# Moving both adaLN products of the first layer's opening onto TensorE in column form

## The chip, the cores and the metric

The kernel runs on one core of a Trainium2 chip. The metric is device microseconds (us) of one launch; lower is better. The engines are TensorE (PE, with its weight loads as PEld), VectorE (DVE), ScalarE (ACT), GpSimd (POOL) and SyncE (SP), which here only issues transfers.

## The reference

A trunk of two transformer layers over 256 tokens of width 2048, batch 1, in float32. Each layer has a mixer (layer 0: sparse attention and latent attention side by side; layer 1: forgetting attention) and a SwiGLU network; in front of each stands an RMS norm that the condition `c` modulates. What the change touches is the first of these norms:

```python
cond = silu(c)                                   # (1, 2048)
mod = (cond @ ada_w[i] + ada_b[i])[:, None, :]   # ada_w[i]: (2048, 6*2048)
sh1, sc1, g1, sh2, sc2, g2 = jnp.split(mod, 6, axis=-1)
h = rmsnorm(x, norm_mix[i]) * (1.0 + sc1) + sh1
...                                              # layer 0: y = nsa_mla_mixer(h, ...), first h @ w_in
x = x + g1 * y
h = rmsnorm(x, norm_ffn[i]) * (1.0 + sc2) + sh2
x = x + g2 * swiglu(h, ffn_w1[i], ffn_w3[i], ffn_w2[i])
```

So before the first projection can begin, two products of `cond` with a 2048 x 2048 slice of `ada_w[0]` are needed: the scale `sc1` and the shift `sh1`, 16 MB each.

## The kernel before

All weights stream once from HBM, in units of 1 MB (128 partitions x 2048 floats), through a ring `RAW` of four slots. `Plan` in `make_plan` numbers the units in the order in which SP loads them: kind "w" is a weight unit, "a" a k-tile of `ada_w` that DVE multiplies and adds, "r" one that PE reads raw. `load` waits, before it fills a slot again, until the unit that was in it four units ago has been used (`lo_ready` for w, `ada_used` for a, `row_used` for r).

A weight unit is split in two for float32 precision: ACT writes the rounded part `WHI` (L554), DVE the rest `WLO` (L1427). The activations are split in the same way into `AHI` and `ALO`. A product is then three matmuls of 128x128 by 128x512 (L909, L910, L911) per k-tile and block of 128 tokens. A chunk is 512 output columns, so four weight units.

An "a" unit costs DVE one instruction of 128x2048: `ACC += RAW * COND[kt]` (L1437 for the first k-tile, L1440 for the others). The 16 k-tiles leave 128 partial sums per column, and PE adds them over the partitions: in `finish` for a shift or scale with 16 matmuls of 128x128 by 128x1 (L958, the accumulator as stationary operand, a column of ones as the moving one), for a gate with four matmuls of 128x128 by 128x512 (L954).

The prologue is 32 units, "a" and "r" in turn. The "a" units make the shift (0, SH1) on DVE. The "r" units make the scale (0, SC1) on PE as a row: `COND[:, k]` (128x1) is stationary and four pieces of 128x512 of the unit move (L1100). Between them stand the six pieces of the position bias: DVE compares (`steps`, L1584, 16 small instructions), PE looks up (`bias_piece`, L1091), DVE keeps (L1592). After the last unit DVE copies the row out of PSUM (L1609), PE turns it into a column with 16 matmuls of one partition (L1106), PE sums the shift (L958), DVE makes `SHM` and `GS` (L1460 to L1468), then the inverse root of the mean square of x (L1511 to L1529). Then `norm(0)` works in four groups of 512 columns: ACT scales x (L669), PE transposes it (L973), DVE modulates (L1536), ACT and DVE split it (L565, L1525). Only after the fourth group does ACT begin on the first two weight units.

The first projection `even_in` has seven chunks of four weight units and an eighth (`even_in`, 7) of 88 columns in one unit. Each chunk carries two "a" units of the gate (0, G1), 16 in all; the last two lie in chunk 7. Then `finish((0, G1))` on PE waits for all 16, and DVE adds the sums to `GROW` (L1451). After it come the turned gates (L1122, L1650), the compression's input (L1660) and its products (L1130).

Every trace record counts a float32 matmul with N=512 or N=1 of plain (unsplit) type as two passes; the order of instructions lists it once. So L958's 16 matmuls are x32 in the trace.

Of the kernel before, what the change touches and what calls it, by code (L numbers as in the profile page):

```python
# [25 lines left out]
RING = 4  # L26
# [40 lines left out]
class Unit:  # L67

    def __init__(self, kind, s, n, w_before, a_before, r_before, src=None, nk=0, cols=0, kt0=0):
        self.kind, self.s, self.n, self.w_before, self.a_before, self.r_before = kind, s, n, w_before, a_before, r_before  # L70
        self.src, self.nk, self.cols, self.kt0 = src, nk, cols, kt0
        if kind == "a":
            self.vec, self.kt = ADA_ORDER[n]
# [31 lines left out]
class Plan:  # L105
# [15 lines left out]
    def chunk(self, name, i, weights, ada=0, buf=None):  # L121

        units, done = [], 0
        for j, (src, nk, cols, kt0) in enumerate(weights):
            units.append(self.unit("w", src=src, nk=nk, cols=cols, kt0=kt0))
# [39 lines left out]
class Machine:  # L165

    def __init__(self, nc, t, ctx, known):
# [74 lines left out]
        self.DG = self.L[:, 0, 0, 0:256].rearrange("p (b t) -> p b t", b=2)  # L242
        self.PART = self.RS[:, 2, 4:6]
# [27 lines left out]

    def scaled_rows(self, g):
# [11 lines left out]
    def make_plan(self, t):  # L284
        plan = self.plan = Plan()

        def rows(w, cols, n, per=4, tiles=KT):
# [9 lines left out]
        self.even_in.append(plan.chunk("even_in", 7, [  # L297
            (tuple(win[:, a:b].rearrange("(k p) n -> p k n", p=P) for a, b in ((2560, 2584), (3608, 3672))), KT, 88, 0)], 2))
# [37 lines left out]
        assert plan.a == len(ADA_ORDER) and plan.r == KT + 8  # L336
# [8 lines left out]
        order = [("norm", 0, g) for g in range(4)] + [("even_in", i) for i in range(7)] + [("cmp", 0), ("cmp", 1)]  # L345
# [27 lines left out]
    def sum_bank(self, v):  # L373

        return {(0, SH1): 5, (0, SC2): 7}.get(v, 6)

    def staged_by(self, key):

        return "st_copied" if key[0] in ("norm", "cmp", "mla") or key in [("even_in", i) for i in range(5)] else "st_ready"

    def t_freed_by(self, key):

        if key[0] == "norm" and key[1]:
            return ("tf_ready", key + (None,))
        if key[0] in ("norm",) or key in (("even_in", 5), ("even_in", 6)):
# [13 lines left out]
def sync_program(block, nc, t, out, m):  # L399

    @block.sync
    def _(sp):
        kinds = m.plan.kinds

        def load(u):
# [9 lines left out]
            if u.src is None:  # L415
                (layer, seg), kt = (u.vec, u.kt) if u.kind == "a" else (ADA_ROW, u.n)
# [42 lines left out]
        for at, src in ((V_C, t["c"].rearrange("a (k p) -> (a k) p", p=P)),  # L459
                        (V_MIX, t["norm_mix"].rearrange("a (k p) -> (a k) p", p=P)),  # L460
                        (V_FFN, t["norm_ffn"].rearrange("a (k p) -> (a k) p", p=P)),
                        (V_QN, t["mla_q_norm"].rearrange("a (k p) -> (a k) p", p=P)),
                        (V_KVN, t["mla_kv_norm"].rearrange("a (k p) -> (a k) p", p=P)),
                        (V_FQ, t["fox_q_norm"]), (V_FK, t["fox_k_norm"]), (V_PK, t["nsa_cmp_pos_k"][0])):
            m["vec_full"].tick(sp.dma_start(m.VROWS[0][at:at + src.shape[0], :], src), "all", 16)
        m["vec_full"].tick(sp.dma_start(m.VROWS[1][0:32, :], t["nsa_cmp_pos_v"][0]), "all", 16)
        for i in range(2):
            m["vec_full"].tick(sp.dma_start(m.VROWS[2 + i][0:96, :], t["ada_b"][i].rearrange("(k p) -> k p", p=P)), "all", 16)
        for u in m.prologue[:RING]:
            load(u)  # L470
        pos = t["positions"]
        m["pos_full"].tick(sp.dma_start(m.POST_I, pos[0:1, :].to_broadcast([P, T])), "all", 16)
        m["pos_full"].tick(sp.dma_start(m.PI[:], pos[0].rearrange("(b p) -> p b", p=P), allow_slow_non_contiguous=True), "all", 16)
        for g in range(4):
            m["pos_full"].tick(sp.dma_start(m.RB[32 * g:32 * g + 32, :], t["rel_bias"][:, :]), "all", 16)
        sp.wait_ge(m["zeroed"].sem, m["zeroed"].at("shifted"))
        for g in range(4):
            m["pos_full"].tick(sp.dma_start(m.RBS[32 * g + 1:32 * g + 32, :], t["rel_bias"][0:31, :]), "all", 16)
        for tb in range(2):
            m["x_full"].tick(sp.dma_start(m.X[:, tb, :], t["x"][0, P * tb:P * tb + P, :]), "all", 16)  # L480
        m["x_full"].tick(sp.dma_start(m.GB[:], t["nsa_gate_b"][0:1, :].to_broadcast([P, 24])), "all", 16)
        m["x_full"].tick(sp.dma_start(m.FB[0:16, 0:1], t["fox_f_b"].rearrange("a h -> h a"), allow_slow_non_contiguous=True), "all", 16)
        for u in m.prologue[RING:]:
            load(u)
        load_chunks(m.even_in)
# [47 lines left out]
def scalar_program(block, nc, t, out, m):  # L533

    @block.scalar
    def _(act):
# [122 lines left out]
        def norm(n):  # L659
            root(("norm", n), 2)  # L660
            wait("rs_ready", n)

            def scaled(g):
                if g >= 2:
                    wait("t_done", ("norm", n, g - 2))
                elif ("norm", n, 0) in m.before_batch:
                    wait("t_done", m.before_batch[("norm", n, 0)])
                for tb in range(2):
                    m["st_copied"].tick(A((m.ST, m.S2)[g % 2][:, tb, :], m.X[:, tb, 512 * g:512 * g + 512], ACT.Copy,  # L669
                                          scale=m.RS[:, 3, tb:tb + 1]), ("norm", n, g))  # L670
            scaled(0)
            scaled(1)
            for g in range(4):
                wait("tf_ready", ("norm", n, g))
                split_hi(("norm", n, g), m.AHI[:, 4 * g:4 * g + 4, :], m.TF[:])
                if g < 2:
                    scaled(g + 2)

        wait("vc_ready", 0)
        m["silu_done"].tick(A(m.COND[:], m.VC[:, V_C:V_C + KT], ACT.Silu), "cond")  # L680
        wait("ang_ready", 0)
        m["trig_ready"].tick(A(m.SIN[:], m.ANG[:, 0:2, :], ACT.Sin), 0)
        m["trig_ready"].tick(A(m.COS[:], m.ANG[:, 2:4, :], ACT.Sin), 0)
        wait("x_full", "all")
        for i in range(4):
            x_squares(("norm", 0), i)
        norm(0)

        def even_first(c):  # L690
# [5 lines left out]
            if c.i < 5:  # L696
                wait("t_done", m.before_batch[c.key])
# [196 lines left out]
def tensor_program(block, nc, t, out, m):  # L894

    @block.tensor
    def _(pe):
# [148 lines left out]

        def run(chunks, stat, ready, after=lambda c: None, rows=(0, 1), between=lambda c, j: None):

            for i, c in enumerate(chunks):
# [5 lines left out]
                for j, u in enumerate(c.w):  # L1055
                    if out and c.i == 3 and j >= len(c.w) - 2:
                        if j == len(c.w) - 2:
                            last_two(c, lambda u: stat(c, u), lambda j: [ready(c, j)])
                        continue
# [13 lines left out]
        def norm(n):  # L1073
            for g in range(4):
                staged(("norm", n, g), range(0, 512, P), g % 2, (m.ST, m.S2)[g % 2])

# [7 lines left out]
        def bias_piece(q):  # L1085
            wait("oh_ready", q)
            if q >= 2:
                wait("bias_kept", q - 2)
            for i in range(16):
                for a in range(3):  # L1090
                    ins = mm(m.PS[:, 6 + q % 2, 32 * i:32 * i + 32], m.OH[q % 2][:, i, :], m.TBL[:, a].rearrange("p g h -> p (g h)"),  # L1091
# [3 lines left out]

        wait("silu_done", "cond")
        for k, u in enumerate(m.prologue[1::2]):
            pe.wait_ge(m.raw_full[u.s % RING], 16 * (u.s // RING + 1))
            for q in range(4):
# [1017 lines left out]
```

## Time and profile before

| | us |
|---|---|
| median of 3 runs | 2775.75 (2767.36 to 2777.0) |
| the profiled execution, own time | 2772.71 |
| its span | 2770.8 |
| first product of `even_in` starts | 154.96 |
| PE busy | 2581.2 (93%) |
| DVE busy | 1720.6 (62%) |
| ACT busy | 1020.1 (37%) |

The profiled execution is one run; its own time is 1.9 us above its span and 3.0 us below the median. Busy shares are of the whole span; the prologue is the first 155 us, and the groups of rows below are taken from it and from a few later places where the same instructions stand. The granted TensorE clock is given as a share of full speed: 1.00 is 2.4 GHz, 0.50 is 1.2 GHz.

### The profile page before, as it was taken

The numbers are of one execution on the slowest core, as the hardware profiler recorded it, in microseconds if no ns is written. First come the engines' busy times: TensorE is split into PE (matmuls) and PEld (weight loads), VectorE is DVE, ScalarE is ACT, GpSimd is POOL, SyncE is SP. The second block draws the span as 40 slices with busy tenths as digits, with TensorE's granted clock in tenths as the row PEclk, the third lists the DMA queues.
The fourth block names the chain that finished last, engine by engine and source line by source line (L and its number), as shares of the span: only waits on it lengthen the run. The fifth ranks groups of instructions, "written<-read, shape, count | busy, mean of one in ns | idle before, by whom it ended". The sixth has DMA issues, their size and how long they took to land.

```text
span 2770.8 us, 29298 instructions
## 1 busy us (share of the span) xinstructions
PE 2581.2 (93%) x11766; PEld 2066.2 (75%) x11766; DVE 1720.6 (62%) x1398; ACT 1020.1 (37%) x947; POOL 3.2 (0%) x11
## 2 busy tenths in 40 slices
PE   5789877889999999999997999999999999999998
PEld 1368656567787788878876888878778788888886
DVE  6566637485766766676656666677677654445445
ACT  1033213244433333333344444444443333333333
POOL 0000000000000000000000000000000000000000
PEclk8789978699999999999998999999999999999999
DMA  8758645476687778777876888789678755655553
GB/s 316 284 203 283 199 151 211 152 257 214 234 312 281 265 251 304 268 268 250 296 215 142 230 183 214 188 237 316 225 252 297 262 187 182 196 182 196 183 185 118
DMA packets 255001, 636.54 MB, mean 230 GB/s; under 512 B 16858, under 2 KB 28084, under 8 KB 229428
## 3 DMA queue, kind: packets, MB, share of 16 engines
q1 hardware_dynamic: 254180, 629.89, 69.2%
q0 software_dynamic: 720, 5.24, 0.5%
q8 instruction: 71, 1.16, 0.2%
q14 instruction: 30, 0.25, 0.0%
HBM read 633.00 MB, written 2.10 MB: 229 GB/s over the span
## 4 chain that ended last, share of the span: by engine, by line
PE 83%; DVE 9%; DMA 3%; ACT 2%; issue 2%; SPq 1%; DVEq 0%; ACTq 0%
PE PS L909 24%; PE PS L911 24%; PE PS L910 24%; DVE WLO L1427 3%; DMA RAW<-in_ada_w 2%; DVE ACC L1440 1%; ACT WHI L554 1%; PE PS L1100 1%; PE PS L958 1%; PE PS L973 1%; PE PS L1130 1%; PE PS L954 1%; PE PS L1287 1%; PE PS L1331 1%; DMA RAW<-in_mla_w_ukv 1%
## 5 line engine op out<-in xcount | busy, mean ns | idle before, releaser
L909 PE MATMUL PS<-WHI,AHI 128*128 128x512 f32 x2120 | 835.2, 394 | 27.6 <-DVE WLO L1427 11.3
L911 PE MATMUL PS<-WHI,ALO 128*128 128x512 f32 x2120 | 828.2, 391 | 0.0
L910 PE MATMUL PS<-WLO,AHI 128*128 128x512 f32 x2120 | 827.7, 390 | 0.0
L1427 DVE TENSOR_TENSOR WLO<-RAW,WHI 128x2048 fp32r<-128x2048 f32 (+2 forms) x222 | 503.6, 2270 | 392.7 <-ACT WHI L554 392.3
L554 ACT ACTIVATE WHI<-RAW 128x2048 fp32r<-128x2048 f32 (+2 forms) x222 | 421.2, 1898 | 709.4 <-PE PS L911 650.2
L1921 DVE TENSOR_TENSOR WLO<-RAW,WHI 128x2048 fp32r<-128x2048 f32 x176 | 403.4, 2292 | 361.7 <-ACT WHI L788 361.1
L788 ACT ACTIVATE WHI<-RAW 128x2048 fp32r<-128x2048 f32 x176 | 337.4, 1917 | 590.9 <-PE PS L911 571.0
L909 PEld LDWEIGHTS PS<-WHI,AHI 128*128 128x128 f32 x2120 | 400.0, 189 | 114.4 <-issue 26.7
L911 PEld LDWEIGHTS PS<-WHI,ALO 128*128 128x128 f32 x2120 | 399.5, 188 | 84.2
L910 PEld LDWEIGHTS PS<-WLO,AHI 128*128 128x128 f32 x2120 | 399.6, 188 | 81.0 <-issue 0.2
L909 PE MATMUL PS<-WHI,GHI 128*128 128x512 f32 x960 | 382.1, 398 | 16.2 <-DVE GLO L1525 8.4
L911 PE MATMUL PS<-WHI,GLO 128*128 128x512 f32 x960 | 377.9, 394 | 0.0
L910 PE MATMUL PS<-WLO,GHI 128*128 128x512 f32 x960 | 377.6, 393 | 0.0
L1440 DVE SCALAR_TENSOR_TENSOR ACC<-RAW,COND,ACC 128x2048 f32<-128x2048 f32 x109 | 255.6, 2345 | 9.5 <-DMA RAW<-in_ada_w 8.3
L909 PEld LDWEIGHTS PS<-WHI,GHI 128*128 128x128 f32 x960 | 183.1, 191 | 59.1 <-DVE GLO L1525 10.5
L911 PEld LDWEIGHTS PS<-WHI,GLO 128*128 128x128 f32 x960 | 182.5, 190 | 38.7
L910 PEld LDWEIGHTS PS<-WLO,GHI 128*128 128x128 f32 x960 | 182.7, 190 | 37.8 <-issue 0.5
L1932 DVE SCALAR_TENSOR_TENSOR ACC<-RAW,COND,ACC 128x2048 f32<-128x2048 f32 x60 | 140.7, 2346 | 0.1
L1100 PE MATMUL PS<-RAW,COND 128*1 128x512 f32 x128 | 65.1, 662 | 31.7 <-DMA RAW<-in_ada_w 31.6
L1100 PEld LDWEIGHTS PS<-RAW,COND 128*1 128x1 f32 x128 | 10.5, 89 | 80.6 <-issue 46.9
L725 ACT ACTIVATE L<-L,NM 128x128 f32<-128x128 f32 x80 | 35.4, 444 | 89.3 <-DVE NM L1729 89.2
L973 PE MATMUL PS<-CON,ST 128*128 128x128 f32 (+1 forms) x244 | 35.9, 290 | 17.9 <-ACT ST L669 6.8
(289 smaller groups left out, 1519.3 us busy)
## 6 DMA issues: line engine op xcount, KB each, us to landing
RAW<-in_ffn_w SPq DMA_DIRECT2D x264, 1024.0 KB, 5.2
RAW<-in_ada_w SPq DMA_DIRECT2D x192, 1024.0 KB, 5.6
RAW<-in_fox_w_in SPq DMA_DIRECT2D x64, 1024.0 KB, 8.6
RAW<-in_even_w_in SPq DMA_DIRECT2D x28, 1024.0 KB, 5.3
RAW<-in_even_w_out SPq DMA_DIRECT2D x16, 1024.0 KB, 6.0
RAW<-in_fox_w_out SPq DMA_DIRECT2D x16, 1024.0 KB, 6.3
GROW<-in_ada_b POOLq DMA_DIRECT2D x4, 1024.0 KB, 5.5
RAW<-in_nsa_cmp_w_k SPq DMA_DIRECT2D x4, 1024.0 KB, 6.3
```

The lines of the kernel that those rows point to most:

```text
L554: A(m.w_view(m.WHI, u), m.w_view(m.RAW, u), ACT.Copy).then_inc(m["hi_ready"].sem, 1)
L725: m["exp_done"].tick(A(m.L[:, b, h, cols], m.L[:, b, h, cols], ACT.Exp, bias=m.NM[:, b, j:j + 1], accum_out=m.SM[:, b, j:j + 1]), p)
L788: A(m.WHI[:, (up.w0 + j) % 2, :], m.RAW[:, (up.s0 + s) % RING, :], ACT.Copy).then_inc(m["hi_ready"].sem, 1)
L909: mm(dst(tb), xh, whi[:, k, :], start=first and k == 0, stop=False)
L910: mm(dst(tb), xh, wlo[:, k, :], start=False, stop=False)
L911: ins = mm(dst(tb), xl, whi[:, k, :], start=False, stop=last and k == nk - 1)
L973: ins = turn(dst, src, m.CON[0:n, C_ID:C_ID + n])
L1100: ins = mm(m.PS[0:1, q, :], m.COND[:, k:k + 1], m.RAW[:, u.s % RING, 512 * q:512 * q + 512], start=k == 0, stop=k == KT - 1)
L1427: TT(m.w_view(m.WLO, u), m.w_view(m.RAW, u), m.w_view(m.WHI, u).bitcast(F32), ALU.subtract).then_inc(m["lo_ready"].sem, 1)
L1440: STT(out=acc[:], in0=raw, scalar=m.COND[:, kt:kt + 1], in1=acc[:], op0=ALU.mult, op1=ALU.add).then_inc(m["ada_used"].sem, 1)
L1921: TT(m.WLO[:, (up.w0 + j) % 2, :], m.RAW[:, (up.s0 + s) % RING, :], m.WHI[:, (up.w0 + j) % 2, :].bitcast(F32), ALU.subtract).then_inc(m["l ...
L1932: STT(out=m.ACC[:], in0=m.RAW[:, slot, :], scalar=m.COND[:, col], in1=m.ACC[:], op0=ALU.mult, op1=ALU.add).then_inc(m["ada_used"].sem, 1)
```

## The change

Nothing but the first norm and the places of a few units is changed.

* All 32 units of the prologue are "r": for each k-tile the scale's, then the shift's. PE takes each in column form: 16 blocks of 128x128 of the unit are stationary, `COND[:, kt]` (128x1) moves, and the sums of all 32 units gather in 32 columns of one PSUM bank. DVE's 16 multiply-adds, the copy of the row, its turning (L1106) and the summing of the shift (L958) are gone.
* x is transposed raw, after units 8 and 14 (`x_raw`), and multiplied by its inverse root on DVE into `XG`, beneath the loads; `spread_both` brings the root into rows of 128 partitions with one matmul.
* The bias pieces stand after units 16, 18, ... 26 and use one PSUM bank instead of two.
* The first two weight units are loaded ahead of the last four "r" units, and split before the modulation.
* After the last unit DVE makes `SHM` and `GS`, and modulation and split go k-tile by k-tile; `opening_unit` on PE waits for one k-tile at a time.
* The small inputs are loaded from ACT's queue, not from SP's; x follows the first four units.
* The 16 "a" units of (0, G1) stand in chunks 0 to 6 as 2, 2, 2, 3, 3, 2, 2, and chunk 7 has none.

```diff
-        self.prologue = [plan.unit("ar"[k % 2]) for k in range(2 * KT)]
-        self.even_in = [plan.chunk("even_in", i, rows(win, 512 * i + (24 if i > 4 else 0), 512), 2) for i in range(7)]
+        self.prologue, self.opening = [], []
+        for kt in range(KT):
+            if kt >= KT - 2:
+                src, nk, cols, kt0 = rows(win, 0, 512)[kt - (KT - 2)]
+                self.opening.append(plan.unit("w", src=src, nk=nk, cols=cols, kt0=kt0))
+                self.prologue.append(self.opening[-1])
+            self.prologue += [plan.unit("r", vec=(0, seg), kt=kt) for seg in (SC1, SH1)]
+        self.even_in = [plan.chunk("even_in", i, rows(win, 512 * i + (24 if i > 4 else 0), 512), (2, 2, 2, 3, 3, 2, 2)[i],
+                                   early=self.opening if i == 0 else ()) for i in range(7)]
...
 # PE
+        side = {8: lambda: (x_raw(0), x_raw(1)), 10: spread_both, 14: lambda: (x_raw(2), x_raw(3))}
+        side.update({16 + 2 * q: lambda q=q: bias_piece(q) for q in range(6)})
+        for k, u in enumerate([u for u in m.prologue if u.kind == "r"]):
             pe.wait_ge(m.raw_full[u.s % RING], 16 * (u.s // RING + 1))
-            for q in range(4):
-                ins = mm(m.PS[0:1, q, :], m.COND[:, k:k + 1], m.RAW[:, u.s % RING, 512 * q:512 * q + 512], start=k == 0, stop=k == KT - 1)
-            m["row_used"].tick(ins, k)
-            if k % 2 and 3 <= k <= 13:
-                bias_piece((k - 3) // 2)
-        wait("row_kept", 0)
-        for j in range(KT):
-            ins = mm(m.PS[:, 4, j:j + 1], m.XT[0:1, j // 2, P * (j % 2):P * (j % 2) + P], m.ONE[0:1, 0:1], start=True, stop=True)
-        m["row_turned"].tick(ins, 0)
-        finish((0, SH1))
-        wait("modulated", 0)
-        norm(0)
+            for j in range(KT):
+                at = KT * (u.vec[1] == SH1) + j
+                ins = mm(m.PS[:, 6, at:at + 1], m.RAW[:, u.s % RING, P * j:P * j + P], m.COND[:, u.kt:u.kt + 1],
+                         start=k == j == 0, stop=k == 2 * KT - 1 and j == KT - 1)
+            m["row_used"].tick(ins, ("ada", k))
+            if k in side:
+                side[k]()
...
+        def opening_unit(c, j):
+            u = c.w[j]
...
+            pe.wait_ge(m["lo_ready"].sem, u.n + 1)
+            for k in range(4):
+                kt = u.kt0 + k
+                wait("lo_split", ("norm", 0, kt))
...
 # ACT
+        for u in m.opening:
+            hi(u)
+        wait("gs_ready", 0)
+        for kt in range(KT):
+            m["hi_split"].tick(A(m.AHI[:, kt, :], m.XG[:, kt, :], ACT.Identity, scale=m.GS[:, 0, kt:kt + 1], bias=m.SHM[:, 0, kt:kt + 1]), ("norm", 0, kt))
...
 # DVE
+        for u in m.opening:
+            lo(u)
+        wait("row_used", ("ada", 2 * KT - 1))
+        modulate(0, SH1, 0, m.PS[:, 6, KT:2 * KT])
+        modulate(0, SC1, 0, m.PS[:, 6, 0:KT])
+
+        def modulated(kt):
+            if kt >= 4:
+                wait("lo_split", ("norm", 0, kt - 4))
+            m["tf_ready"].tick(TS(m.TF[:, kt % 4, :], m.XG[:, kt, :], m.GS[:, 0, kt:kt + 1], m.SHM[:, 0, kt:kt + 1], ALU.mult, ALU.add), ("norm", 0, kt))
+        modulated(0)
+        for kt in range(KT):
+            if kt + 1 < KT:
+                modulated(kt + 1)
+            wait("tf_ready", ("norm", 0, kt))
+            split_lo(("norm", 0, kt), m.ALO[:, kt, :], m.TF[:, kt % 4, :], m.AHI[:, kt, :])
```

How PE's instructions stand in a row from its first transposes to the first product. The kernel before; L1100 is the scale's row, L1091 the bias, L1106 the row's turning, L958 the shift's sums:

```order
L1081 MATMUL PS<-CON,TF 128x96 x2
L1100 MATMUL PS<-RAW,COND 1x512 x16
L1091 MATMUL PS<-GROW,ST 128x32 x48
L1100 MATMUL PS<-RAW,COND 1x512 x8
...
L1100 MATMUL PS<-RAW,COND 1x512 x16
L1106 MATMUL PS<-CON,XT 128x1 x16
L958 MATMUL PS<-CON,ACC 128x1 x16
L973 MATMUL PS<-CON,ST 128x128 x8
L973 MATMUL PS<-CON,S 128x128 x8
...
L909 MATMUL PS<-WHI,AHI 128x512
```

PE at the same place after the change; L1133 is the column form of scale and shift, L1119 the transposes of x, L1124 the spreading of the root, L1105 the bias:

```order
L1095 MATMUL PS<-CON,TF 128x96 x2
L1133 MATMUL PS<-COND,RAW 128x1 x144
L1119 MATMUL PS<-CON,X 128x128 x16
L1133 MATMUL PS<-COND,RAW 128x1 x32
L1124 MATMUL PS<-L,CON 128x256
L1133 MATMUL PS<-COND,RAW 128x1 x64
L1119 MATMUL PS<-CON,X 128x128 x16
L1133 MATMUL PS<-COND,RAW 128x1 x32
L1105 MATMUL PS<-GROW,ST 128x32 x48
...
L1133 MATMUL PS<-COND,RAW 128x1 x80
L1058 MATMUL PS<-WHI,AHI 128x512
```

Sixteen units of four wide matmuls have become 32 units of 16 matmuls of one column; the row's turning and the transposes of the scaled x no longer stand between the last unit and the first product.

On DVE, after the change, from the last kept bias piece to the first units of the projection (L1605 and L1625 bias, L1454 `WLO`, L1637 modulation, L1552 `ALO`, L1464 and L1467 the gate's "a" units):

```order
L1605 COPY BIAS<-PS 128x64x8 x2
L1625 TENSOR_TENSOR BIAS<-BIAS,CON 128x8x128 x2
L1454 TENSOR_TENSOR WLO<-RAW,WHI 128x2048 x2
L1487 TENSOR_TENSOR SHM<-PS,VC 128x16
L1489 COPY IDLE<-SHM 128x1
L1493 TENSOR_TENSOR MD<-PS,VC 128x16
L1495 SCALAR_TENSOR_TENSOR GS<-MD,VC 128x16
L1637 TENSOR_SCALAR TF<-XG,GS,SHM 128x256 x2
L1552 TENSOR_TENSOR ALO<-TF,AHI 128x256
...
L1464 TENSOR_SCALAR ACC<-RAW,COND 128x2048
L1454 TENSOR_TENSOR WLO<-RAW,WHI 128x2048 x2
```

The two weight units are split ahead of the modulation, and the third weight unit waits behind all 16 k-tiles and one "a" unit.

## Rows read from the trace of the kernel before

**Rows 1.** The page: granted TensorE clock in 40 equal slices of the span.
```profile
PEclk8789978699999999999998999999999999999999
```
**Rows 2.** Windows: start:end, length, busy PE, PEld, DVE, ACT, POOL (count), clock, DMA, GB/s.
```profile
40.00:110.00 70.00, 57.14 (x391) 15.65 (x390) 55.02 (x99) 0.00 (x0) 0.00 (x0) 0.94 0.95 373
115.50:121.20 5.70, 5.70 (x32) 5.70 (x32) 0.00 (x0) 0.00 (x0) 0.00 (x0) 0.61 1.00 407
121.20:128.20 7.00, 7.00 (x33) 6.92 (x33) 0.00 (x0) 0.00 (x0) 0.00 (x0) 0.50 0.06 23
128.20:155.00 26.80, 7.65 (x34) 6.49 (x33) 17.03 (x35) 13.04 (x15) 0.00 (x0) 0.50 0.00 0
155.00:157.50 2.50, 2.50 (x6) 2.02 (x7) 2.50 (x2) 0.00 (x0) 0.00 (x0) 0.50 0.62 146
157.60:180.00 22.40, 22.40 (x100) 18.50 (x99) 9.74 (x5) 7.35 (x4) 0.00 (x0) 1.00 0.78 281
```
**Rows 3.** Windows of L958 alone, the column form, at three places.
```profile
121.20:128.20 7.00, 6.97 (x32) 6.90 (x32) 0.50 0.06 23
520.30:527.30 7.00, 6.99 (x32) 6.90 (x32) 0.50 0.44 152
1377.80:1381.50 3.70, 3.63 (x32) 3.54 (x31) 1.00 1.04 385
```
**Rows 4.** Windows of all engines: L958 after dense products, and what follows it.
```profile
1437.40:1441.00 3.60, 3.60 (x34) 3.60 (x33) 2.45 (x2) 2.80 (x4) 0.00 (x0) 1.00 1.03 163
1441.00:1444.00 3.00, 3.00 (x9) 2.39 (x9) 2.64 (x3) 0.44 (x2) 0.00 (x0) 0.53 1.01 149
```
**Rows 5.** Timeline from the last unit to the first product: start, length, engine, line.
```profile
109.46 3.59 PE L1100 MATMUL PS<-RAW,COND 128*1 128x512 f32 x8 [1.43 <-DMA RAW<-in_ada_w]
...
128.26 0.17 DVE L1460 TENSOR_TENSOR SHM<-PS,VC 128x16 f32<-128x16 f32 x1 [12.82 <-PE PS L958]
...
129.07 0.15 DVE L1614 COPY MD<-GS 128x1 f32<-128x1 f32 x1
...
132.44 1.94 PE L973 MATMUL PS<-CON,ST 128*128 128x128 f32 x8 [4.22 <-ACT ST L669]
...
136.35 1.06 ACT L565 ACTIVATE AHI<-TF 128x1024 fp32r<-128x1024 f32 x1 [2.83 <-DVE TF L1536]
137.51 1.23 DVE L1525 TENSOR_TENSOR ALO<-TF,AHI 128x1024 fp32r<-128x1024 f32 x1 [1.19 <-ACT AHI L565]
...
154.96 0.77 PE L909 MATMUL PS<-WHI,AHI 128*128 128x512 f32 x1 [9.87 <-DVE WLO L1427]
```
**Rows 6.** Timeline: the start, a bias piece, and DVE in the first chunk.
```profile
5.63 2.07 SPq L417 DMA_DIRECT2D RAW<-in_ada_w  x4
...
9.19 0.22 ACT L680 ACTIVATE COND<-VC 128x16 f32<-128x16 f32 x1 [7.16 <-DVE VC L1545]
...
13.24 9.28 PE L1100 MATMUL PS<-RAW,COND 128*1 128x512 f32 x16 [4.72 <-DMA RAW<-in_ada_w]
...
46.09 1.36 PE L1091 MATMUL PS<-GROW,ST 128*128 128x32 bf16 x48
...
156.93 1.28 DVE L1437 TENSOR_SCALAR ACC<-RAW,COND 128x2048 f32<-128x2048 f32 x1
164.03 2.29 DVE L1427 TENSOR_TENSOR WLO<-RAW,WHI 128x2048 fp32r<-128x2048 f32 x1 [5.83 <-ACT WHI L554]
```
**Rows 7.** Timeline of DVE at the end of `even_in`.
```profile
324.70 4.80 DVE L1440 SCALAR_TENSOR_TENSOR ACC<-RAW,COND,ACC 128x2048 f32<-128x2048 f32 x2
329.42 0.41 DVE L1622 COPY TF<-PS 88x256 f32<-88x256 f32 x1
...
336.11 0.69 DVE L1451 TENSOR_TENSOR GROW<-PS,GROW 128x512 f32<-128x512 f32 x1 [0.34 <-PE PS L954]
```
**Rows 8.** Timeline of PE at the same place.
```profile
319.64 1.04 PE L973 MATMUL PS<-CON,ST 128*128 128x128 f32 x8
329.56 6.51 PE L954 MATMUL PS<-ACC,CON 128*128 128x512 f32 x8 [8.88 <-DVE ACC L1440]
```

More of the change, by code:

```diff
@@ L458, in _ @@
         m["con_full"].tick(sp.dma_start(m.CON[:], t["const_table"][:, :]), 0, 16)
[L459 to L468, printed above, removed]
         for u in m.prologue[:RING]:
             load(u)
[L471 to L478, printed above, removed]
         for tb in range(2):
             m["x_full"].tick(sp.dma_start(m.X[:, tb, :], t["x"][0, P * tb:P * tb + P, :]), "all", 16)
[L481 to L482 removed]
         for u in m.prologue[RING:]:
             load(u)
[L485 removed]
+        for c in m.even_in:
+            for u in c.units:
+                if u not in m.opening:
+                    load(u)
         for u in m.cmp_in[0]:
@@ L657, in enter @@
             keep_x(n, 3)
[L659 to L677, printed above, removed]
+        for at, src in ((V_C, t["c"].rearrange("a (k p) -> (a k) p", p=P)),
+                        (V_MIX, t["norm_mix"].rearrange("a (k p) -> (a k) p", p=P)),
+                        (V_FFN, t["norm_ffn"].rearrange("a (k p) -> (a k) p", p=P)),
+                        (V_QN, t["mla_q_norm"].rearrange("a (k p) -> (a k) p", p=P)),
+                        (V_KVN, t["mla_kv_norm"].rearrange("a (k p) -> (a k) p", p=P)),
+                        (V_FQ, t["fox_q_norm"]), (V_FK, t["fox_k_norm"]), (V_PK, t["nsa_cmp_pos_k"][0])):
+            m["vec_full"].tick(act.dma_start(m.VROWS[0][at:at + src.shape[0], :], src), "all", 16)
@@ L681, in _ @@
+        wait("x_full", "all")
+        for i in range(4):
+            x_squares(("norm", 0), i)
+        root(("norm", 0), 2)
         wait("ang_ready", 0)
@@ L1093, in bias_piece, with x_raw, spread_both @@
             m["bias_sum"].tick(ins, q)
+        def x_raw(g):
+            if g == 0:
+                wait("x_full", "all")
+            if g >= 2:
+                wait("xg_ready", g - 2)
+            for j in range(4):
+                for tb in range(2):
+                    at = 512 * g + P * j
+                    ins = turn(m.x_turned(g)[:, j, P * tb:P * tb + P], m.X[:, tb, at:at + P], m.ID)
+            m["t_done"].tick(ins, ("norm", 0, g))
+        def spread_both():
+            wait("diag_ready", 0)
+            m["spread_done"].tick(mm(m.PS[:, 5, 0:T], m.ONE, m.DGF, start=True, stop=True), 0)
@@ L1115, in even_after @@
                 staged(c.key, (0, P) if c.i in (3, 4) else range(0, 512, P))
-        run(m.even_in, lambda c, u: halves(m.AHI, m.ALO, u.kt0), lambda c, j: ("lo_split", ("norm", 0, j)), even_after)
+        run(m.even_in, lambda c, u: halves(m.AHI, m.ALO, u.kt0), lambda c, j: None, even_after)
         finish((0, G1))
@@ L1648, in _ @@
         wait("gk_turned", 0)
+        wait("bias_full", "all")
         gk = m.PS[:, 4, 0:T].rearrange("p (b n) -> p b n", b=2)
```

116 lines of the change are left out of this document (61 added, 55 removed).

## The prediction

> **What bounds the kernel now.** I read the page first. The granted clock in 40 slices shows that the kernel is a PE kernel with a weak spot at its beginning: the first three slices and the sixth to eighth are at 8 tenths or below [rows 1]. The prologue is the first 155 us, so it has to be read by itself, in windows. From 40 to 110 us the 16 DMA engines are 95% busy at 373 GB/s, PE is busy for 57 of 70 us and DVE for 55: the loads bound that part [rows 2]. At 373 GB/s a unit of 1.05 MB takes 2.8 us, so the 32 units can't be had in less than 90 us. From 113 us on the transfers no longer matter (23 GB/s, then none), and what runs is a chain: the last row unit ends at 113.05, the first product starts at 154.96, 41.9 us later [rows 2, 5]. In that chain PE stands at half clock from the row's turning to the first product and 2.5 us beyond [rows 2].
>
> The change takes that chain out, and pays for it with work on PE: that is the trade to be costed.
>
> **The column form, the term that decides.** A unit in row form is 8 passes and takes 3.59 us at full clock [rows 5]. The column form of a unit is 16 matmuls of 128x128 by 128x1, in 32 passes. It is not in the prologue before, but the same instruction is: L958 sums an accumulator of 128x2048 with a column of ones, with the same shapes and types. It takes 3.63 us at full clock and 6.97 to 6.99 at half [rows 3]. So at full clock a column unit costs what a row unit costs, and everything hangs on the clock.
>
> What does the clock do under this form? In 115.5 to 121.2 PE is busy all the time with L1106 (one column moving), the window begins partly at full clock (0.61 in the mean), and the clock falls and stays at 0.50 through the 7.0 us of L958 that follow without a gap [rows 2]. That is 12.7 us of an engine that is 100% busy by the record, and the clock is not raised. At 520.3 the same: 7.0 us at 0.50 [rows 3]. Where L958 comes on a fast PE it runs at 3.6 us, and the clock is at 0.53 in the 3 us behind it, though dense products run there [rows 4]. So no row shows this form raise the clock, and two show it lost. Against this the dense products: half clock at 155.0 to 157.5, full from 157.6 [rows 2]. In the changed kernel nothing dense stands before or between the 32 units. I take half clock for all of them: 32 x 6.99 = 223.7 us. The other end is 32 x 3.63 = 116.2 us.
>
> The Trainium skill speaks against this reading: by "TensorE: Matmul & The Clock Gate", Part 1, the engine's own recent busyness releases the throttle, and column units in an unbroken row leave no idle time. By that the term would be the 116 us of the other end. The two windows at 115.5 and 121.2 don't agree with it, busy throughout and at half. It is the first rival below.
>
> **The rest of PE's row.** Four batches of eight transposes: 1.94 us each at half clock [rows 5], 7.8 us. The root's spreading: one matmul of 256 columns, two passes, about half a row-form pass of 0.85 us at half clock each (the first 16 passes took 9.28 us, mostly at half [rows 6]): 0.9 us. Six bias pieces: 1.36 us each at full clock [rows 6]; at half clock the trace has none. They are no cheaper than 1.36 and, since every other PE form doubles, no dearer than 2.7; I take 2.0, between, since 48 matmuls of 32 columns at 28 ns are partly bound by issue: 12.0 us, with ends 8.2 and 16.3. Each piece also waits for DVE, but two column units (14 us) lie between pieces, and DVE's part is one keep of 1.0 and 16 compares of 4.2 us: hidden.
>
> The start: before, `COND` is ready at 9.41 and PE begins on the first row unit at 13.24, when its load has landed [rows 6]. Now the loads are issued some 4 us before their 5.63 [rows 6], since SP issues the constants and then them, and the small inputs compete with them from ACT's queue. Not before 9.4, not after 16; I take 12.0, near the 13.24. The loads themselves are no bound at 6.99 us a unit against 2.8.
>
> Sum: 12.0 + 223.7 + 7.8 + 0.9 + 12.0 = 256.4 us for the end of the last unit, where 113.05 was. This is 143 us later.
>
> **The chain behind it.** `SHM` and `GS` take 0.8 us (128.26 to 129.07) [rows 5]. Then ACT's 128x256 `AHI`: a quarter of the 1.06 us form plus a fixed part, 0.4; DVE's `ALO`, from the 1.23 us form, 0.4 [rows 5]. The weight units are split already. First product at 256.4 + 1.7 = 258.1, where 154.96 was: **+103.1 us**. The 41.9 us of the chain are gained but for 1.7; the 143 us more than eat them.
>
> Behind the first product: DVE now has 16 times a modulation (about 0.3) and a split (0.4), 11 us, before the "a" unit (1.28) and `WLO` of the third weight unit (2.29) [rows 6]: ready 14.4 us after the first product. PE's first two units are 48 products, 2.5 us at half clock and the rest at 0.227, 12.2 us (0.227 from 100 passes in 22.4 us from 157.6 on [rows 2]). PE waits **+2.2 us**; ends 0 and 4. Before, it did not wait there.
>
> At the end of `even_in` PE stands idle for 8.88 us [rows 8] until DVE has done the two last "a" units (4.80 us), which start at 324.70 behind the second split; then PE's sums take 6.51 us [rows 8], and DVE's last addition ends at 336.80 [rows 7]. Those two units are now in chunks 3 and 4, where DVE has room: it is busy 9.7 of 22.4 us in the first chunk [rows 2], and a third "a" adds 2.35. So PE can begin at 320.7, after its transposes [rows 8]; the first two sums wait for nothing, the last two for DVE's additions after 324.7 + 0.4: 325.1 + 4 x 0.7 and two handovers, about 328.5. **-8.3 us**; ends 0 (if the compression's weights or a later DVE step are late next) and -10.
>
> Sum against the span: 103.1 + 2.2 - 8.3 = +97.0; 2770.8 + 97.0 = 2867.8, and with the 1.9 us around the span 2869.7. The median of before is 3.0 above the profiled time, so the forecast of **2870** could be met from 2870 to 2873 by that alone.
>
> **The rivals.** *Full clock throughout.* Continuous column work holds PE at 1.00, as in the 3.6 us of 1437.4 and 1377.8 [rows 3, 4]. Then 12.0 + 116.2 + 4 x 0.9 + 0.4 + 8.2 = 140.4, first product 142.1: -12.9. The opening runs fast from the start, 10.9 us against DVE's 14.4, a wait of 3.5 less 1.3 won: +2.2. With -8.3: -19.0, a time of 2754, faster. It decides from the point where the clock is granted for over about 85% of the units. For it: the full-clock rows of L958. Against it: they begin on a clock that was high already, and one is followed at once by a fall.
>
> *Lifts.* Bias pieces and transposes, dense in columns for a moment, raise the clock for a while. If each of the eight side batches gives one column unit at 3.63 instead of 6.99, 27 us are won: 2843; with two each, 54: 2816. Against it: eight transposes twice (132.4 to 136.1) and all of `norm(0)` lie in 128.2 to 155.0 at 0.50 [rows 2, 5].
>
> *DMA-bound as now.* The units follow the loads at 2.8 us, the sum is 12 + 90, first product near 110. Both prices of the column unit are above 2.8, so I give it nothing.
>
> **How the numbers follow.** Half clock throughout 0.83, lifts 0.08, full clock 0.09. The forecast's own range: start -2.6 to +4, bias -3.8 to +4.3, opening -2.2 to +1.8, end of `even_in` -1.7 to +8.3, so 2859 to 2888, and up to 3 us for the median. Down to 2842 it takes in the mildest lifts; full clock and the strong lifts stay out, some 14 in 100. Range 2842 to 2892. Over 0.5% (14 us), about what a measurement of this kernel can tell from no change: faster 0.09, same 0.01, slower 0.90.
>
> **What would show it.** In the changed profile: the column form x1024 in the first 257 us, about 218 ns a pass, granted clock 0.50 in that window; DMA share near 0.4 there, at 150 GB/s; DVE and ACT mostly idle; the last unit to the first product 1.7 us; the sums of (0, G1) directly behind their transposes. Wrong if the column passes come at 113 ns (the first rival) or if the clock rises after a bias piece (the second); if units take longer than 7 us, then they wait for something that I have not named.

## The result, and the profile after

The changed kernel takes 2857.85 us (median of 4 runs, 2852.24 to 2869.15) against 2776.38 us before (4 runs): a ratio of 1.0305, 95% interval 1.0264 to 1.0346. It is slower by 81 us. The forecast was 2870, with a range of 2842 to 2892. The profiled execution took 2869.15 us with a span of 2867.4, 96.6 us above the span of before.

The prologue in the timeline of the chain that ended last; columns are start, length, engine, line. It answers to [rows 5] and [rows 6]:

```profile
5.10 10.31 DMA TF<-in_ada_b
15.55 1.20 PE PS L1095 x4
16.85 0.53 DVE VC L1558
17.67 61.60 PE PS L1133 x288
79.27 3.52 PE PS L1119 x16
82.78 13.44 PE PS L1133 x64
96.23 1.06 PE PS L1124 x2
97.29 27.10 PE PS L1133 x128
124.39 3.52 PE PS L1119 x16
127.90 13.44 PE PS L1133 x64
141.35 1.30 PE PS L1105 x48
142.65 13.63 PE PS L1133 x64
...
216.01 1.30 PE PS L1105 x48
217.32 34.12 PE PS L1133 x160
252.28 0.66 DVE TF L1637 x2
253.56 0.77 PE PS L1058
```

From 17.67 us on every piece is PE's own, with no wait between: 288 passes in 61.60 us are 213.9 ns a pass, 6.84 us a unit. That is the half-clock price of [rows 3]. All 1024 passes of L1133 take 217.9 us, 6.81 us a unit in the mean. The transfers set the pace before, at 373 GB/s [rows 2]. From 17.7 to 251.4 us they now give 156 GB/s in the mean, at a DMA share of 0.44; at the end, where the first weight units are loaded too, it is 0.68 (windows of all engines; busy us of PE, PEld, DVE, ACT, POOL, then clock, DMA share, GB/s):

```profile
17.70:78.90 61.20, 61.20 (x287) 61.20 (x288) 16.39 (x78) 8.18 (x21) 0.00 (x0) 1.00 0.43 147
217.10:251.40 34.30, 34.30 (x169) 34.24 (x164) 7.97 (x5) 1.91 (x1) 0.66 (x1) 1.00 0.68 244
```

From the last unit to the first product the timeline shows what the change was made of, and it works as written:

```profile
251.46 0.17 DVE L1487 TENSOR_TENSOR SHM<-PS,VC 128x16 f32<-128x16 f32 x1 [18.06 <-PE PS L1133]
...
252.07 0.17 DVE L1495 SCALAR_TENSOR_TENSOR GS<-MD,VC 128x16 f32<-128x16 f32 x1
252.28 7.99 ACT L687 ACTIVATE AHI<-XG,SHM,GS 128x256 fp32r<-128x256 f32 x16 [21.20 <-DVE GS L1495]
252.28 0.73 DVE L1637 TENSOR_SCALAR TF<-XG,GS,SHM 128x256 f32<-128x256 f32 x2
252.98 0.43 DVE L1552 TENSOR_TENSOR ALO<-TF,AHI 128x256 fp32r<-128x256 f32 x1
```

The last unit ends at 251.4 and the first product starts at 253.56: 2.1 us where 41.9 us stood. The chain that the change removes is really gone. It is outweighed by a prologue that ends 138 us later.

At the end of `even_in` the long wait of [rows 8] is cut in two, one short piece of work on each side of a smaller wait (PE; the bracket is idle time before and who ended it):

```profile
420.46 1.88 PE L954 MATMUL PS<-ACC,CON 128*128 128x512 f32 x4
425.92 3.58 PE L954 MATMUL PS<-ACC,CON 128*128 128x512 f32 x4 [3.57 <-DVE GROW L1478]
```

### The profile page after: what moved, and what is told of

It is laid out like the page before. It is cut to its first block, busy times and chain, and to the rows that moved or that the text cites. A ratio compares the mean times of both kernels' runs of the same rounds, so it can differ in the third digit from the quotient of the medians.

```text
span 2867.4 us, 30943 instructions
## 1 busy us (share of the span) xinstructions
PE 2726.7 (95%) x12600; PEld 2267.2 (79%) x12600; DVE 1686.1 (59%) x1398; ACT 1021.8 (36%) x953; POOL 3.2 (0%) x11
## 4 chain that ended last, share of the span: by engine, by line
PE 87%; DVE 8%; ACT 2%; issue 1%; DMA 1%; ACTq 0%; SPq 0%; DVEq 0%
PE PS L909 23%; PE PS L911 23%; PE PS L910 23%; PE PS L1133 8%; DVE WLO L1454 2%; ACT WHI L549 1%; DVE ACC L1467 1%; PE PS L973 1%; PE PS L1157 1%; PE PS L958 1%; PE PS L1314 1%; PE PS L1358 1%; PE PS L1210 1%; PE PS L954 1%; DMA RAW<-in_mla_w_ukv 0%
## 5 line engine op out<-in xcount | busy, mean ns | idle before, releaser
L909 PE MATMUL PS<-WHI,AHI 128*128 128x512 f32 x2088 | 821.7, 394 | 19.8 <-DVE ALO L1908 9.6
L911 PE MATMUL PS<-WHI,ALO 128*128 128x512 f32 x2088 | 814.4, 390 | 0.0
L910 PE MATMUL PS<-WLO,AHI 128*128 128x512 f32 x2088 | 814.3, 390 | 0.0
L1454 DVE TENSOR_TENSOR WLO<-RAW,WHI 128x2048 fp32r<-128x2048 f32 (+2 forms) x222 | 503.7, 2270 | 389.7 <-ACT WHI L549 389.4
L909 PEld LDWEIGHTS PS<-WHI,AHI 128*128 128x128 f32 x2088 | 393.2, 188 | 104.8 <-issue 16.5
L911 PEld LDWEIGHTS PS<-WHI,ALO 128*128 128x128 f32 x2088 | 392.9, 188 | 82.6
L910 PEld LDWEIGHTS PS<-WLO,AHI 128*128 128x128 f32 x2088 | 393.1, 188 | 79.5 <-issue 0.2
L1467 DVE SCALAR_TENSOR_TENSOR ACC<-RAW,COND,ACC 128x2048 f32<-128x2048 f32 x94 | 220.5, 2345 | 0.4 <-issue 0.3
L1133 PEld LDWEIGHTS PS<-COND,RAW 128*128 128x128 f32 x1024 | 219.5, 333 | 1.4 <-ACT COND L665 1.2
L1133 PE MATMUL PS<-COND,RAW 128*128 128x1 f32 x1024 | 219.4, 352 | 0.9 <-ACT COND L665 0.9
L1961 DVE SCALAR_TENSOR_TENSOR ACC<-RAW,COND,ACC 128x2048 f32<-128x2048 f32 x60 | 140.8, 2346 | 0.1
L1846 DVE TENSOR_TENSOR TF<-PS,GROW 128x1024 f32<-128x1024 f32 x28 | 34.2, 1222 | 23.1 <-PE PS L911 23.1
```

Of the source, the lines that this page charges most:

```text
L909: mm(dst(tb), xh, whi[:, k, :], start=first and k == 0, stop=False)
L910: mm(dst(tb), xh, wlo[:, k, :], start=False, stop=False)
L911: ins = mm(dst(tb), xl, whi[:, k, :], start=False, stop=last and k == nk - 1)
L1133: ins = mm(m.PS[:, 6, at:at + 1], m.RAW[:, u.s % RING, P * j:P * j + P], m.COND[:, u.kt:u.kt + 1], start=k == j == 0, stop=k == 2 * KT - 1 ...
L1454: TT(m.w_view(m.WLO, u), m.w_view(m.RAW, u), m.w_view(m.WHI, u).bitcast(F32), ALU.subtract).then_inc(m["lo_ready"].sem, 1)
L1467: STT(out=acc[:], in0=raw, scalar=m.COND[:, kt:kt + 1], in1=acc[:], op0=ALU.mult, op1=ALU.add).then_inc(m["ada_used"].sem, 1)
```

## The experiments

**The changed kernel again, for a second profile.** No edit.

> The changed kernel as it is, a second profile of it. Theory (the column form runs at half clock): the 1024 passes of L1133 again at 213 ns from start to start, 6.83 us a unit, first product near 253.6 us, time between 2850 and 2870 us. If instead the clock rises now and then in the prologue, which would be the cause of the spread from 2852 to 2869 us, some of the units take 3.6 us and the first product comes 5 us or more earlier.

Measured: 2860.61 us (4 runs, 2858.98 to 2863.88), ratio 1.0314 (1.0297 to 1.0331). First product at 250.0. PE's column passes are at 213 ns except in one place, right behind the 16 transposes of `x_raw`:

```profile
78.69 3.40 PE L1119 MATMUL PS<-CON,X 128*128 128x128 f32 x16
81.93 10.75 PE L1133 MATMUL PS<-COND,RAW 128*128 128x1 f32 x64
```

and in windows of all engines:

```profile
81.90:85.30 3.40, 3.40 (x33) 3.40 (x31) 0.00 (x0) 0.00 (x0) 0.00 (x0) 0.97 0.32 133
85.30:247.00 161.70, 161.70 (x1010) 161.52 (x1010) 34.37 (x79) 3.82 (x2) 0.66 (x1) 0.50 0.48 163
```

The length of the 64 passes shows the lift, 10.75 us against 13.65 elsewhere; the 0.97 of the first window stands almost wholly ahead of this trace's first record. So the second rival, the lifts, exists: here once, for 3.4 us, worth 2.9 us. Behind it PE works for 162 us without a wait, six bias pieces and 16 more transposes among the column units, and stays at 0.50. The first profile has no lift. A lift of this size doesn't explain the spread from 2852 to 2869 us: the two profiles differ by 8.7 us, 3.6 of it ahead of the first product, 3.4 in the attention stage (from its first scores, L1210, to L1010, the root's spreading of the next norm: 285.3 and 281.9 us) and 1.8 behind.

**Dense products added to the column units.**

```diff
             for j in range(KT):
+                if j % 4 == 3:
+                    mm(m.PS[:, 4, :], m.IDB[:], m.CON[:, 0:256].bitcast(BF16), start=True, stop=True)
                 at = KT * (u.vec[1] == SH1) + j
```

> The changed kernel with work added: in each of the 32 column units, four matmuls of 128x128 by 128x512 (bf16, result not used) in the place after every fourth block. Theory (the column form doesn't raise the clock, dense products do): the granted clock goes to 1.00 within the first units, a unit takes 3.63 us plus 4 x 0.21 us = 4.5 us instead of 6.83, first product near 180 us, time near 2857 - 74 = 2783 us. Rival (four dense products a unit are too few, or PE's column passes are slow for another reason, as reading RAW while transfers write it): 6.83 + 4 x 0.43 = 8.5 us a unit, time near 2912 us.

Measured: 2884.26 us (2882.83 to 2886.96), ratio 1.0397 (1.0380 to 1.0414), so slower than the changed kernel by 26 us. My expectation fell, and the rival's price of 8.5 us a unit and 2912 us was too high. The passes keep their half-clock pace with one wide product after every four blocks:

```profile
37.81 0.59 PE L1134 MATMUL PS<-CON,IDB 128*128 128x512 bf16 x1
38.19 1.71 PE L1135 MATMUL PS<-COND,RAW 128*128 128x1 f32 x8
39.76 0.59 PE L1134 MATMUL PS<-CON,IDB 128*128 128x512 bf16 x1
```

Eight column passes take 1.57 us from start to the wide product, 196 ns each, and the unit 7.8 us. There is one exception, as in the profile before: behind the second 16 transposes, from 141 to 144 us, eight passes take 0.8 us, and then the half-clock pace is back, wide products or not. The run says that a sprinkle of dense work is paid for and gives nothing back; it doesn't yet tell the clock from another reason for slow passes. The next two do.

**The scale back in row form, in turn with column units.** (L1133 is now the row form, L1136 the column form; the row is copied and turned at the end as before the change. The transposes of x come in four batches of eight instead of two of 16, and the bias pieces one unit later.)

```diff
-            for j in range(KT):
-                at = KT * (u.vec[1] == SH1) + j
-                ins = mm(m.PS[:, 6, at:at + 1], m.RAW[:, u.s % RING, P * j:P * j + P], m.COND[:, u.kt:u.kt + 1], ...)
+            if u.vec[1] == SC1:
+                for q in range(4):
+                    ins = mm(m.PS[0:1, q, :], m.COND[:, u.kt:u.kt + 1], m.RAW[:, u.s % RING, 512 * q:512 * q + 512], ...)
+            else:
+                for j in range(KT):
+                    ins = mm(m.PS[:, 6, KT + j:KT + j + 1], m.RAW[:, u.s % RING, P * j:P * j + P], m.COND[:, u.kt:u.kt + 1], ...)
```

> The changed kernel with one thing undone: the scale's 16 units in row form (4 matmuls of 128x1 by 128x512), the shift's still in column form, both on PE, in turn; the row is turned at the end as before. Theory (the column form neither raises nor holds the clock, the row form does both): row units at 3.6 us; the column units between them at 3.6 us if the row unit before them is enough to hold the clock, so 7.2 us a pair, first product near 155 us, time near 2762 us; if each column unit loses it, rows and columns at half clock, 13.7 us a pair, first product near 259 us, time near 2866 us. Rival (the column passes are slow by themselves in this place): row units 3.6 us, column units always 6.8 us, 10.4 us a pair, first product near 206 us, time near 2813 us.

Measured: 2795.02 us (2 runs, 2791.52 and 2798.52), ratio 1.0086 (1.0062 to 1.0111): 63 us faster than the changed kernel, with the same bytes, the same number of units on PE, and 9 us more at the end for copying and turning the row. First product at 187.2. PE in the timeline:

```profile
96.81 3.59 PE L1133 MATMUL PS<-RAW,COND 128*1 128x512 f32 x8
100.34 3.73 PE L1136 MATMUL PS<-COND,RAW 128*128 128x1 f32 x32
...
105.21 5.29 PE L1133 MATMUL PS<-RAW,COND 128*1 128x512 f32 x8
110.43 3.73 PE L1136 MATMUL PS<-COND,RAW 128*128 128x1 f32 x32
114.03 1.35 PE L1105 MATMUL PS<-GROW,S 128*128 128x32 bf16 x48
115.31 5.29 PE L1133 MATMUL PS<-RAW,COND 128*1 128x512 f32 x8
120.53 3.73 PE L1136 MATMUL PS<-COND,RAW 128*128 128x1 f32 x32
```

and the windows of the pair at 105.2:

```profile
105.20:110.40 5.20, 5.20 (x12) 0.77 (x8) 5.04 (x17) 0.00 (x0) 0.00 (x0) 0.67 0.49 186
110.40:114.00 3.60, 3.60 (x33) 3.57 (x33) 0.00 (x0) 0.00 (x0) 0.00 (x0) 1.00 0.69 225
```

This is none of the three prices that I had written down, and it is the clearest reading of the case. A column unit, loaded through the same ring and read from RAW like those of the changed kernel, runs in 3.7 us, so the passes are not slow by themselves: the third case falls. The row unit pays instead. It starts at half clock (0.67 in the mean of its window), and the clock rises under it; the column unit behind it runs at 1.00, and the next row unit mostly starts at half again. Such a pair takes 8.8 us and a bias piece 1.3. Some pairs, where the column unit too lost part of the clock, took up to 10.7. At 96.81, once, the row unit began at full clock, and that pair took 7.1.

**Row and column mixed within a pair.** The same work, in another order: one row matmul, four column blocks, four times.

```diff
+            for q in range(4):
+                ins = mm(m.PS[0:1, q, :], m.COND[:, a.kt:a.kt + 1], m.RAW[:, a.s % RING, 512 * q:512 * q + 512], ...)
+                for j in range(4 * q, 4 * q + 4):
+                    ins = mm(m.PS[:, 6, KT + j:KT + j + 1], m.RAW[:, b.s % RING, P * j:P * j + P], m.COND[:, b.kt:b.kt + 1], ...)
```

> As the coarse mixture of row and column units, but interleaved within a pair: one row matmul of 512 columns, then four column blocks, four times. Theory: dense and column work alternate every microsecond, so that the clock sees the same in any stretch; if it is held, 7.2 us a pair and a time near 2762 us; if not, 13.7 us a pair and near 2866 us. Whether it agrees with the coarse mixture tells whether the place of the dense work matters or only its share.

Measured: 2850.67 us (2847.14 and 2854.19), ratio 1.0287 (1.0262 to 1.0312); first product at 249.3. From 17.15 to 74.6 us the pieces repeat without a change: two row passes in 1.8 us, eight column passes in 1.8 us, both at the half-clock price, 14.4 us a pair. The clock rises only around the transposes and some bias pieces, for 3 to 14 us at a time; there the pieces take 1.0 us each (L1135 is the row form, L1139 the column form):

```profile
17.15 1.86 PE L1135 MATMUL PS<-RAW,COND 128*1 128x512 f32 x2 [0.93 <-ACT COND L665]
18.94 1.87 PE L1139 MATMUL PS<-COND,RAW 128*128 128x1 f32 x8
...
106.80 1.02 PE L1135 MATMUL PS<-RAW,COND 128*1 128x512 f32 x2
107.75 1.05 PE L1139 MATMUL PS<-COND,RAW 128*128 128x1 f32 x8
```

Between this run and the one before it the work is the same; what differs is where the row matmuls stand, and that a pair waits for both of its units and frees them later. The second costs little: PE waits 6.3 us for loads here, 1.8 us there, of the 62 us between the first products (249.3 and 187.2) and the 56 us between the medians. The rest is the clock. It rose under every row unit that began at half when the row work stood in one block; in slices it stayed at half for the first 57 us, and rose later only behind transposes and bias pieces.

**The small vectors on SP, ahead of the units.**

```diff
         m["con_full"].tick(sp.dma_start(m.CON[:], t["const_table"][:, :]), 0, 16)
+        for at, src in ((V_C, t["c"]...), ...):
+            m["vec_full"].tick(sp.dma_start(m.VROWS[0][at:at + src.shape[0], :], src), "all", 16)
+        ...                                    # and no longer from ACT's queue
         for u in m.prologue[:RING]:
```

> The changed kernel with the small vectors loaded from SP ahead of the first units, as before the change. Theory (the condition is late because its rows share the DMA engines with 4 MB of units and 2 MB of x): COND ready near 10.5 us instead of 17.6, first column unit near 12 to 13 us when its load has landed, time 4 to 6 us below the changed kernel. Rival (the start is hidden by the loads): within 2 us.

Measured: 2857.88 us (4 runs, 2847.82 to 2860.07), ratio 1.0301 (1.0277 to 1.0326). In the trace the start is what was expected, and more: the vectors have landed at 7.2 instead of 15.5, the first column unit begins at 10.74 instead of 17.67, the first product at 246.6 instead of 253.6 or 250.0:

```profile
7.23 1.19 PE L1095 MATMUL PS<-CON,TF 122*128 122x122 f32 x4 [7.23 <-DMA TF<-in_ada_b]
10.74 61.57 PE L1133 MATMUL PS<-COND,RAW 128*128 128x1 f32 x288 [2.32 <-DMA RAW<-in_ada_w]
```

In the time the 3 to 7 us can't be seen; in this profile the attention stage took 288.4 us, 3.1 more than in the first profile of the changed kernel, and what follows it 5.3 less. So the price of the start is shown, its worth in the whole is not. The edit changes the queue and the order together; which of the two counts, the run doesn't tell.

**The kernel before with the gate's units moved, alone.**

```diff
-        ... rows(win, 512 * i + ..., 512), 2) for i in range(7)]
+        ... rows(win, 512 * i + ..., 512), (2, 2, 2, 3, 3, 2, 2)[i]) for i in range(7)]
-            (tuple(...), KT, 88, 0)], 2))
+            (tuple(...), KT, 88, 0)]))
```

> The kernel before with one part of the change alone: the 16 units of the gate (0, G1) in chunks 0 to 6 as 2, 2, 2, 3, 3, 2, 2, none in chunk 7. Theory: PE's 8.9 us wait before L954 goes, the compression's products start 6 to 8 us earlier, and 6 to 8 us less in all: near 2769 us. Rival: the gain is given back in the attention stage, whose waits are for transfers: within 2 us of before.

Measured: 2768.48 us (10 runs) against 2774.0, ratio 0.9985 (0.9971 to 0.9999). From the first product to the compression's first (L1130) it is 178.3 us, before 184.1: 5.8 us less. PE:

```profile
324.22 1.88 PE L954 MATMUL PS<-ACC,CON 128*128 128x512 f32 x4
329.68 3.58 PE L954 MATMUL PS<-ACC,CON 128*128 128x512 f32 x4 [3.57 <-DVE GROW L1451]
336.33 4.02 PE L1130 MATMUL PS<-RAW,BF 128*30 128x256 f32 x10 [2.92 <-DVE BF L1660]
```

The wait of 8.88 us becomes one of 3.57, since DVE frees the bank of the first sum only after its split of chunk 6. In the time it is 4 to 6 us, and the interval nearly reaches none. This profile also shows how far stages move that no edit touched: its first product starts at 158.0 instead of 155.0, its attention stage is 3.1 us longer than before's and what follows it 6.6 us shorter.

**A hybrid: the new chain, the old prologue's arithmetic.** The scale in row form on PE, the shift on DVE, as before; x turned and scaled beneath the loads, modulation and split k-tile by k-tile, weight units early, gate units moved; the small vectors ahead of the units on SP's queue, as before. Two of DVE's multiply-adds stand ahead of the position work.

```diff
-            self.prologue += [plan.unit("r", vec=(0, seg), kt=kt) for seg in (SC1, SH1)]
+            self.prologue += [plan.unit("a"), plan.unit("r", vec=(0, SC1), kt=kt)]
```

> A hybrid: the change's chain behind the prologue (x turned and scaled beneath the loads, weight units split early, k-tile by k-tile, gate units moved), but the scale in row form on PE and the shift on DVE as before, two multiply-adds of DVE ahead of the position work. Theory: units follow the loads at 5.6 us a pair, the last one ends near 105 us, then the shift's sums (3.6 to 7 us), the row's turning (5.8 us), modulation and split: first product near 120 us, 35 us earlier than before; with 7 us from the gate units near 2776 - 42 = 2734 us. Rival: DVE, which has 16 multiply-adds, 96 compares and now the scaling of x, sets the pace, and the last unit ends at 113 us or later: 2745 us or more.

Measured: 2746.65 us (4 runs, 2742.35 to 2748.93), ratio 0.9896 (0.9879 to 0.9912): faster than both. First product at 130.0, not 120. The last row unit begins at 115.0 where I had expected about 105. DVE has room, idle for 5.0 and 4.8 us; what is late is a transfer. So the time is that of my rival (2745 us or more), and the cause is another:

```profile
103.14 2.35 DVE L1471 SCALAR_TENSOR_TENSOR ACC<-RAW,COND,ACC 128x2048 f32<-128x2048 f32 x1 [5.02 <-DMA RAW<-in_ada_w]
105.41 2.28 DVE L1458 TENSOR_TENSOR WLO<-RAW,WHI 128x2048 fp32r<-128x2048 f32 x1
112.53 2.35 DVE L1471 SCALAR_TENSOR_TENSOR ACC<-RAW,COND,ACC 128x2048 f32<-128x2048 f32 x1 [4.83 <-DMA RAW<-in_ada_w]
```

The last "a" unit goes into the slot of the early weight unit, so SP can't issue it until DVE has split that weight unit (107.7), which in turn stands behind an "a" unit that landed at 103.1.

**The hybrid with the weight units last.**

```diff
-            if kt >= KT - 2:
-                ...
-                self.prologue.append(self.opening[-1])
...
+        self.prologue += self.opening                       # behind the last of the 32 units
...
+        lo(m.opening[0])
         finish((0, SH1))
+        lo(m.opening[1])
         wait("row_turned", 0)
```

> The hybrid once more, with the two weight units loaded behind the last of the 32 units instead of ahead of the last four, split beneath the shift's sums and the row's turning, and a third multiply-add ahead of the norm's root on DVE. Theory (in the first hybrid the early weight units made SP wait for DVE's split, 115.0 us for the last unit where 105 was possible): last unit begins near 106 us, first product near 120 us, 10 us less than the first hybrid: near 2737 us. Rival (DVE's own work is the pace): no more than 3 us less.

Measured: 2735.22 us (4 runs, 2731.96 to 2744.32), ratio 0.9875 (0.9848 to 0.9902), 11 us below the first hybrid, or 9 us when each is set against the kernel before in its own series (36.4 and 27.4 us below it). The last unit begins at 105.88 and the first product at 122.3. The loads are back at their pace, and the split of the two weight units lies under PE's sums and the turning of the row (windows of all engines):

```profile
15.00:110.00 95.00, 76.30 (x456) 22.12 (x454) 78.28 (x169) 9.62 (x22) 0.66 (x1) 0.95 0.96 368
109.40:122.20 12.80, 11.16 (x65) 11.05 (x64) 8.54 (x11) 4.17 (x5) 0.00 (x0) 0.62 1.04 408
```

Of the 12.8 us that remain, 11.2 are again the column form (L957, 4.25 us) and one-partition matmuls (L1139, 6.98 us), on a clock that is 0.62 in the mean of that window.

## Why the prediction was right, point by point

| term | forecast | profile after |
|---|---|---|
| start of the first unit | 12.0 | 17.7 |
| 32 column units | 223.7 | 217.9 |
| transposes and spreading | 8.7 | 8.1 |
| six bias pieces | 12.0 | 7.8 |
| end of the last unit | 256.4 | 251.4 |
| to the first product | 1.7 | 2.1 |
| first product, against before | +103.1 | +98.6 |
| opening | +2.2 | about +1 |
| end of `even_in` | -8.3 | -5.8 (alone, on the kernel before) |
| attention stage and behind | 0 | +3.1 |
| span | +97.0 | +96.6 |

In the profile after, opening and end of `even_in` can be read only together: from the first product to the compression's first it is 179.0 us, before 184.2, so -5.2.

*The column form at half clock* carried the forecast, and it holds: 6.81 us a unit in the mean of all 32, where the rows of L958 said 6.99. Those rows include the tail of the last pass, 0.16 us, which overlaps the next unit here; taken 32 times that is most of the 5.8 us by which the term was too high. That the clock is the reason, and not the passes' place or their operands, is shown by the coarse mixture: the same unit at 3.7 us behind a row unit. What it is in this form that leaves the clock at half is not shown.

*The first rival*, full clock because PE is never idle, is out. It rested on the Trainium skill's rule ("TensorE: Matmul & The Clock Gate", Part 1), that recent busyness releases the throttle. PE's busy share is 100% from 17.7 to 251.4 us, and the clock is at half, but for 3.4 us in one of two profiles: the measurement decides, and an engine can be fully busy by the record and still be at half clock.

*The second rival*, lifts, was put at 8 in 100 with at least 27 us. It was seen at 2.9 us in one profile of the changed kernel, and at some 3 us in the run with dense products added; the other profile and that of the run with the vectors on SP have none. I wrote that nothing dense stands between the 32 units, though the transposes do, and argued that those of `norm(0)` had never raised the clock. That was not enough: behind 16 of them it rose twice, and in the fine mixture it rose behind batches of eight.

*The bias pieces* were mis-sized, 12.0 against 7.8. I assumed that they would double like all else, at least in part; at half clock a piece is 1.44 us long, where it was 1.36 before [rows 6], and it adds 1.30 us to the chain.

*The start* was mis-sized the other way, 12.0 against 17.7 and beyond my bound of 16: the vectors' rows were issued by 5.6 us and landed only at 15.4. From 5.6 to 15.4 the DMA engines were fully busy (414 GB/s) with 6 MB of units and x. The kernel before had issued the vectors from 1.2 to 5.6 us, ahead of its first unit at 5.63 [rows 6].

*The sum* agrees with the span to 0.4 us, and that is luck. The start was 5.7 us too low; the column units were 5.8 and the bias pieces 4.2 too high. Behind the first product the gain was 5.2 us, not 6.1, and the attention stage took back 3.1 that the sum did not have. What the prediction can claim is the half clock and its price, to 3%, and with it the direction and the size.

*A reading that was wrong* without a consequence: I wrote that from 113 us on the transfers no longer matter, at 23 GB/s. By [rows 2] they still ran at 407 GB/s from 115.5 to 121.2 us, and the 23 hold from 121.2 on. No term used it.

*The opening.* I expected PE to wait 2.2 us for the third weight unit. It doesn't wait. `WLO` is ready at 266.4, 12.8 us after the first product and not 14.4, since DVE's 16 modulations and splits took 9.3 us from there and not 11. PE comes to it at 266.83, 13.3 us after the first product and not 12.2, because its first 11 products, not 6, were still at half clock. What I had as a wait is about 1 us of slower products.

*The end of even_in.* The first two sums went where I said; the handover was longer, since DVE's first addition waits for the split that ends at 424.8, and PE's last two sums wait for it. 5.8 us, not 8.3.

*Profile and median.* I made the sum against one profile, and it met that profile's span. The median of the runs is 11 us lower. The profiled execution is the slowest of four; its attention stage was 3.1 us longer than before's and there was no lift. Among the ten profiles of this study the attention stage takes 281.5 to 288.4 us without any change to it, and what stands behind it 2081.8 to 2092.3, which I had given nothing for: a forecast from one profile carries that much by itself. What sets it was not tried; in windows of 10 us the granted clock of the attention stage moves between 0.50 and 1.00 many times, and not in the same places before and after.

## What to carry to other kernels

Before work is moved onto TensorE in the shape of many stationary blocks with one moving column, look up what the same shape costs at half clock, and ask what is dense around it; in a stretch of its own it ran at 6.84 us instead of 3.6 us per 1 MB unit here, twice the price and 2.4 times the load's. If such work can't be avoided, set it behind a block of dense work and keep it short: 12 of 16 column units kept the full clock for their 3.7 us behind a row unit. And take a large change apart: here the chain behind the loads was worth 25 to 33 us, and the arithmetic moved to feed it cost 138 us; kept apart, the gain stays, at 2735 us.

When units share a ring, an early load that is drained late holds the slot of a critical one: the last unit began 9.1 us later in the first hybrid than in the second, and the first product 7.7 us later. The second hybrid also moved one multiply-add on DVE, so the split of the two is not shown, but the wait for the transfer behind the held slot is in the trace.

## What the runs showed of the hardware that was not expected

* The order of the same work decides the clock: row and column units in blocks took 8.8 us a pair, in slices 14.4 us wherever no transposes or bias pieces had raised the clock.
* 48 bf16 matmuls of 128x128 by 128x32 are 1.44 us long at half clock and 1.36 at full, so their pace (28 to 30 ns each) is hardly the clock's.
* Wide bf16 products between column blocks, one after every four, cost 1.0 us a unit and did not raise the clock.
* 11 small transfers of vectors from ACT's queue, issued within 4.8 us, landed 9.8 us after the last issue beside 6 MB from SP's queue; issued first from SP's queue they had landed 1.6 us after it.
